# Two transformer blocks on one core: an earlier or later place for three small steps of the experts

## The reference

```python
def peer(xn, w_query, sub_keys, expert_u, expert_v):     # per block of 128 tokens
    q = (xb @ w_query).reshape(128, 8, 2, 128)
    s = einsum('thpc,pkc->thpk', q, sub_keys)
    s1, i1 = top_k(s[:, :, 0], 16); s2, i2 = top_k(s[:, :, 1], 16)
    sc, ci = top_k(s1[..., :, None] + s2[..., None, :], 16)    # of 256 sums
    e = i1[ci // 16] * 128 + i2[ci % 16]                 # one of 16384 experts
    g = softmax(sc)
    act = gelu(einsum('td,thkd->thk', xb, expert_u[e]))
    return einsum('thk,thkd->td', g * act, expert_v[e])
# second block:
    x = x + peer(rms_norm(x, norm2_g), ...)
    return rms_norm(x, final_norm_g)
```

## Time and profile before

| | |
|---|---|
| time, median of 3 runs | 1314.31 us (1312.51 to 1314.51) |
| profiled execution, its own time | 1314.31 us |
| its span, first to last instruction | 1312.5 us |
| mean granted TensorE clock | 0.997 of full speed |
| TensorE busy | 1287.2 us, 98% of the span |
| weight loads of TensorE | 1172.3 us, 89% |
| VectorE / ScalarE / GpSimd busy | 936.6 / 694.5 / 33.8 us |
| transfers | 260.56 MB, mean 199 GB/s |
| last u matmul / first v matmul start | 955.78 / 957.33 us |
| last matmul starts | 1305.43 us |

### The profile page before, as it was taken

The page is one execution under the profiler, slowest core; times in us unless marked ns, Lnnn a source line. Parts: engine busy times, 40 slices in busy tenths (PEclk is TensorE's granted clock), DMA queues, the critical chain, the costliest instruction groups (busy, mean ns, idle before and its releaser), DMA issues.

```text
span 1312.5 us, 22031 instructions
## 1 busy us (share of the span) xinstructions
PE 1287.2 (98%) x8615; PEld 1172.3 (89%) x8615; DVE 936.6 (71%) x1699; ACT 694.5 (53%) x1162; POOL 33.8 (3%) x27
## 2 busy tenths in 40 slices
PE   9999999999999898999999999999999999999997
PEld 8899989998878688999999999999988888888886
DVE  6676567764457655999989777777766666666666
ACT  5565457664455645444454455555554444555554
POOL 0000031000020001000000000000000000000000
PEclk9999999999999999999999999999999999999999
DMA  7443455556656335477777665655677766666663
GB/s 268 156 134 107 140 182 180 188 180 192 192 163 217 112 113 181 145 222 228 231 233 228 204 200 191 201 186 194 203 256 276 242 241 240 240 241 241 242 241 110
DMA packets 72807, 260.56 MB, mean 199 GB/s; under 512 B 8256, under 2 KB 9024, under 8 KB 72448
## 3 DMA queue, kind: packets, MB, share of 16 engines
q1 hardware_dynamic: 71232, 255.25, 59.3%
q0 software_dynamic: 1040, 3.34, 0.8%
q10 hardware_dynamic: 432, 0.56, 0.1%
HBM read 240.25 MB, written 18.87 MB: 197 GB/s over the span
## 4 chain that ended last, share of the span: by engine, by line
PE 91%; ACT 4%; DVE 3%; issue 2%; ACTq 0%; DVEq 0%
PE ps L1072 26%; PE ps L476 14%; PE ps L484 14%; PE ps L485 14%; PE ps L486 14%; PE ps L1055 2%; PE ps L530 1%; ACT whi L1109 1%; PE ps L517 1%; DVE wlo L1590 1%; PE ps L523 1%; ACT TH L1115 1%; PE ps L511 1%; PE ps L999 1%; PE ps L494 0%
## 5 line engine op out<-in xcount | busy, mean ns | idle before, releaser
L1590 DVE TENSOR_TENSOR wlo<-raw,whi 128x1024 fp32r<-128x1024 f32 (+2 forms) x410 | 497.8, 1216 | 309.7 <-ACT whi L1109 307.5
L1109 ACT ACTIVATE whi<-raw 128x1024 fp32r<-128x1024 f32 (+2 forms) x421 | 441.8, 1051 | 414.2 <-PE ps L1072 168.6
L484 PE MATMUL ps<-TH,whi 128*128 128x256 f32 x1504 | 433.0, 288 | 0.0
L485 PE MATMUL ps<-TL,whi 128*128 128x256 f32 x1504 | 426.1, 283 | 0.0
L486 PE MATMUL ps<-TH,wlo 128*128 128x256 f32 x1504 | 426.0, 283 | 0.0
L485 PEld LDWEIGHTS ps<-TL,whi 128*128 128x128 f32 x1504 | 289.1, 192 | 0.0
L484 PEld LDWEIGHTS ps<-TH,whi 128*128 128x128 f32 x1504 | 289.0, 192 | 0.0
L486 PEld LDWEIGHTS ps<-TH,wlo 128*128 128x128 f32 x1504 | 288.8, 192 | 0.0
L1072 PE MATMUL ps<-whi,TH 128*128 128x512 f32 x512 | 199.4, 389 | 1.3 <-issue 1.3
L1072 PE MATMUL ps<-whi,TL 128*128 128x512 f32 x512 | 199.3, 389 | 0.0
L1072 PE MATMUL ps<-wlo,TH 128*128 128x512 f32 x512 | 199.3, 389 | 0.0
(11 more groups left out here) (327 smaller groups left out, 1393.8 us busy)
## 6 DMA issues: line engine op xcount, KB each, us to landing
raw<-in_expert_u_dram SPq DMA_DIRECT2D x128, 512.0 KB, 3.7
raw<-in_expert_v_dram SPq DMA_DIRECT2D x128, 512.0 KB, 3.6
raw<-in_w_up_dram SPq DMA_DIRECT2D x32, 512.0 KB, 3.6
raw<-in_w_down_dram SPq DMA_DIRECT2D x32, 512.0 KB, 4.2
acts<-stage SPq DMA_DIRECT2D x32, 512.0 KB, 4.0
stage<-acts SPq DMA_DIRECT2D x30, 512.0 KB, 3.3
raw<-in_w_in_dram SPq DMA_DIRECT2D x20, 512.0 KB, 4.4
raw<-in_w_gate_dram SPq DMA_DIRECT2D x16, 512.0 KB, 3.5
```

Of the source, the lines that this page charges most:

```text
L484: e.matmul(dst, whi[:, h, sl], xh[:, k, :], start=k == 0, stop=False)
L485: e.matmul(dst, whi[:, h, sl], xl[:, k, :], start=False, stop=False)
L1109: e.activation(whi[:, u % NH, 0:n], raw[:, u % NR, 0:n], ACT.Copy).then_inc(*hi(u))
L1590: e.tensor_tensor(wlo[:, u % NH, 0:n], raw[:, u % NR, 0:n], whi[:, u % NH, 0:n].bitcast(F32), ALU.subtract).then_inc(*lo(u))
```

## The change

It moves instructions; it adds and removes none, apart from semaphore values that follow the new order.

1. TensorE: the products of groups 0 and 1 stood behind the 24 matmuls of unit 66. They now stand behind the first 12 of unit 67; group 2 stays behind unit 67. The loop body became the function `weigh`.
2. VectorE, turn 127: takes 0, 1, 2 and cut 0 now stand ahead of the split of `EV + 1`; cut 1, take 3, cut 2 behind it. On ScalarE the text changes but the order is the same.
3. VectorE, last norm, t = 1: the order was x10, v1, g10, x11, g11 and is now x10, g10, x11, v1, g11. For t = 0 it stays x00, x01, v0, g00, g01.

```diff
         end_d = signal("end_d", (
-            "x00 x01 v0 g00 g01 r0 out01 x10 v1 g10 x11 g11 r1 out11").split())
+            "x00 x01 v0 g00 g01 r0 out01 x10 g10 x11 v1 g11 r1 out11").split())
...
+            def weigh(g):
+                e.wait_ge(*hot.at(g))
+                if g < 4:
+                    if g == 0:
+                        e.wait_ge(*route_a.at("turned0"))
+                    if g == 1:
+                        e.wait_ge(*route_d.at("turned1"))
+                    if g == 2:
+                        e.wait_ge(*route_d.at("turned2"))
+                else:
+                    e.wait_ge(*weight_a.at(g - 4))
+                for i in range(4):
+                    for w in (2, 3):
+                        m = e.matmul(ps[g % 4][:, i * 128:i * 128 + 128], room[:, g % 2, 0, i, :], room[:, g % 2, w, i, :],
+                                     start=w == 2, stop=w == 3)
+                m.then_inc(*weighed(g))
...
                 m = cols(EU + n, 0, 8, TH, TL, ps[b][:, 0:256], range(4))
                 if n == 127:
                     m.then_inc(*half_used("u"))
+                if n == HOT_FROM + 1:
+                    for g in hot_groups(HOT_FROM):
+                        weigh(g)
                 cols(EU + n, 0, 8, TH, TL, ps[b][:, 0:256], range(4, 8)).then_inc(*used(EU + n))
-                for g in hot_groups(n):
-                    e.wait_ge(*hot.at(g))
...
-                    m.then_inc(*weighed(g))
+                if n > HOT_FROM:
+                    for g in hot_groups(n):
+                        weigh(g)
...
                 take_weights(hot_groups(n - 1))
                 if n == 1:
                     score(3)
-                split(EU + n + 2)
                 if n == 127:
+                    split(EV + 1)
                     for i in range(3):
                         cut(i)
+                else:
+                    split(EU + n + 2)
...
                     one_hots(g)
                 if n == 1:
                     score(3)
-                split(EU + n + 2)
                 if n == 127:
-                    take(0)
                     for i in range(3):
-                        take(i + 1)
-                        cut(i)
+                        take(i)
+                    cut(0)
+                    split(EV + 1)
+                    cut(1)
+                    take(3)
+                    cut(2)
+                else:
+                    split(EU + n + 2)
...
             for t in range(2):
                 part, v, s, r = end_st[t]
                 last_sum(t, 0)
-                if t == 0:
-                    last_sum(t, 1)
+                if t == 1:
+                    last_gain(t, 0)
+                last_sum(t, 1)
                 e.wait_ge(*end_a.at(f"{t}0"))
                 mean_eps(v, part[:, 0:1], 1024).then_inc(*end_d(f"v{t}"))
-                last_gain(t, 0)
-                if t == 1:
-                    last_sum(t, 1)
+                if t == 0:
+                    last_gain(t, 0)
                 last_gain(t, 1)
```

## The result

| | before | changed |
|---|---|---|
| time, median (19 runs each) | 1313.03 us | 1310.96 us |
| lowest and highest run | 1312.3, 1318.05 | 1308.94, 1313.18 |
| span of the profiled execution | 1312.5 | 1307.8 |

The ratio is 0.9976, with a 95% interval of 0.9969 to 0.9983: 3.1 us less, give or take 0.9. It is not the ratio of the two medians, which lie 2.07 apart (the means: 1313.85 and 1310.58, 3.28 apart). The runs of each kernel lie in groups, and the median jumps from one to the other: ten of 19 runs before are at 1313.03 or under, nine of 19 changed ones at 1309.75 or under, and the next lies at 1310.96. The spans of the two profiled executions differ by 4.7 us, which is more. The two traces together say where each part of that is.

The account below looks back on a forecast made before the run. TensorE, busy 98% of the span, bounds the kernel, then a short serial chain after its last matmul. 0.91 + 1.43 + 0.05 + 0.73 = 3.1 us off 1314.31 gives 1311.2 us, range 1309.1 to 1312.9.

Parts of the forecast that it names:

- Part 1, 0.91 us: Groups 0 and 1 amid unit 67: 0.91 us gained of 1.21 lost in TensorE's waits; bounds 0.8 to 1.21.
- The short wait for hot(2): TensorE at group 2: a new wait of about 0.3 us, because VectorE's pair for group 2 does not move.
- Interrupting unit 67 costs nothing: TensorE in unit 67: as many switches between one-hot products and u matmuls as before, so priced at nothing.
- Part 2, 1.43 us: Turn from u to v: first weighted values ready before TensorE wants them at 955.90, so the 1.43 us stop goes.
- The chain: Turn 127: takes from 953.81, ScalarE's cut(0) 954.73, VectorE's 955.17 to 955.59, a margin of 0.3 us.
- The first v unit, 0 to 0.14, taken as 0.05: First 12 v matmuls take 2.86 against a mean of 2.72; 0 to 0.14 us may return, 0.05 taken.
- Part 3, 0.73 us: Last norm: with g10 directly after x10, x11 starts at 1305.96, not 1306.69; 0.73 us gained, bounds 0.6 to 0.73.
- v1 behind x11 cost nothing: Last norm: v1 is done by 1306.8, while the root also needs x11's square, which starts at 1306.64 and lasts about 0.6.
- No part failed: Rival, chance 0.15 together: cut(0) still late (1312.6), or the wait moves to VectorE's pairs in units 67 and 68 (1311.7).
- The pair for group 3: VectorE, part 1: hot(3) is ready 0.8 us before its time; 0.5 late would leave part 1 only 0.4.
- The slower case: Rival, chance 0.02: in the v stage the load of EV+5 lands late; a landing of 13.8 us gives 1314.6.
- The chances: Whole kernel: faster 0.65, same 0.32, slower 0.03, with 0.2% (2.6 us) as what can be told from no change.

Follow-up runs that it names:

- best: Changed kernel with both fills, and group 2 moved amid unit 68 as well: median 1307.53 us, ratio to before 0.9952.
- margin: Changed kernel with two more VectorE one-hot comparisons ahead of take(0): last u matmul to first v matmul 0.76 us, against 0.12 changed; no run time given.
- split_second: Changed kernel with turn 127's split of EV+1 after takes 0 to 2 but ahead of cut 0: last u to first v matmul 0.77 us; no run time given.
- fb: Kernel before with filling matmuls of no use in two TensorE gaps (8 near 133, 17 near 448): median 1311.19 us, 8 runs.
- fc: Changed kernel with both sets of filling matmuls, same kernel as fills, run beside fb on one chip: median 1307.93 us, 5 runs.
- p1_only: Kernel before with part 1 of the change alone: median 1313.14 us, ratio to before 0.9997.
- p2_only: Kernel before with part 2 of the change alone (VectorE's turn 127): median 1312.75 us, ratio to before 0.9992.
- p3_only: Kernel before with part 3 of the change alone (the last sum): median 1313.3 us, ratio to before 0.9996.
- groups_late: Changed kernel with groups 0 and 1 behind the whole of unit 67: unit 66's last matmul to group 2 5.13 us, against 4.26 changed; no run time given.
- f133: Changed kernel with only the 8 filling matmuls near 133: median 1309.98 us, 8 runs.
- fp2: Kernel before with part 2 of the change and both sets of filling matmuls: median 1309.71 us, 11 runs.
- fills: Changed kernel with filling matmuls in two TensorE gaps (8 near 133, 17 near 448): median 1307.75 us, ratio to before 0.9953, 5 runs.

## Why the prediction was right, step by step

The forecast was 1311.2 us, 3.1 less. Measured: 1310.96, and by the ratio 3.1 less, or 3.26 without the clock's scatter. The gain was worked out. That the absolute time agrees to 0.2 is luck: the forecast started from 1314.31, the median of three runs, and over 19 runs the median before is 1313.03. From there 3.1 less is 1309.9; the changed kernel's median lies higher because it fell into the upper group of its runs.

- *Part 1, 0.91 us.* Measured 0.91, in the change and alone. The start at 748.59 was forecast for group 0, 1.55 after unit 66's last matmul; it is 1.56. The short wait for hot(2) is there as forecast (0.2 in the view of the waits, 0.36 for the weight loads of the same group); best, where group 2 stands amid unit 68, shows that it is worth 0.3.
- *Interrupting unit 67 costs nothing.* Right: from group 0 to group 2 there is nothing that the sum doesn't have.
- *Part 2, 1.43 us.* Measured 1.43. The chain stood where it was forecast: takes 0.70 after ScalarE's last copy of a group starts (forecast 0.63), ScalarE's cut 1.54 after (1.55), VectorE's cut 1.99 (1.99), its end 0.31 before TensorE wants it (0.31). margin and split_second show by both sides that it is this chain that counts.
- *The first v unit, 0 to 0.14, taken as 0.05.* It is 2.75 in place of 2.83, so 0.08. The 2.86 of the forecast was the length of the window (957.30 to 960.16), not of the unit, which starts at 957.33; so the excess over the mean was 0.11 and not 0.14. The return of all of it, which the prediction drew from the Trainium skill (TensorE: Matmul & The Clock Gate, section "Step-by-step: what each phase is for"), did not happen: even with no stop the first unit is 0.03 slower than the mean. No run here shows why.
- *Part 3, 0.73 us.* The mechanism is right and the size was 0.1 too small: 0.83, outside the bounds of 0.6 to 0.73. I took the release of the last sum as 0.53 after the matmul's start, from the first bank's row. It is 0.43 at most: x11 starts when VectorE is free of g10 (1301.36 + 0.61), no later. With the gain out of the way the release could be earlier still; no run here shows how early. The first bank's sum again starts 0.53 after its last matmul in the changed kernel (1296.77 to 1297.30); why the last bank's comes sooner is open. v1 behind x11 cost nothing, as forecast: it ends at 1302.73 and the root starts at 1303.52.
- *The rivals.* No part failed. The pair for group 3 is ready at 751.73 + 0.69 = 752.42, 0.8 before the group starts (753.23), as forecast. The slower case had no sign: the store that stands behind the load of EV+5 was issued at 954.77, so the load was out by then, and TensorE has no wait in the v stage.
- *The chances.* The gain was expected at 0.5 above the 0.2% that the prediction took for what can be told from no change. It came out near there: 0.24%, with an interval of 0.17 to 0.31%. That is clear of no change, but it reaches below the 0.2%, so these runs alone don't decide between "faster" (0.65) and "same" (0.32) by that bound.
- *What I had not asked.* I took the scatter of 2 us between runs as given. A good part of it had a cause in the trace, and with that out of the way (fb and fc) a change of 3 us in 1310 stood clear of every single run.

## What to carry to other kernels

When an engine is busy without a gap around a stop, the stop is worth its length, and here each part could be forecast to a tenth of a microsecond. What limits it is the chain that comes next: work it out in the same way before naming a price. Moving a dependent step by half a unit can be right where a whole unit is as bad as none, because a chain in the other direction closes.

When the runs of one kernel lie in groups, look at the granted clock window by window before timing more. Comparing distances inside two traces takes such chance out, as long as no fall of the clock lies within them; comparing spans does not. And where runs lie in groups, the difference of two medians can mislead: here it was 2.07, where the ratio gave 3.1, the means 3.28 and the traces 3.26.

## What the runs showed of the hardware

- The granted clock fell behind a gap of 4.29 us of TensorE in every execution profiled without a fill there (before, changed, p1_only, p2_only, p3_only, margin, split_second, groups_late, f133). Behind one of 2.0 us near 133 it fell in four of eight (before, p1_only, p2_only, split_second) and stayed at 1.00 in the other four. Behind one of 1.7 us near 490 it fell in one of fourteen (fp2), at no cost that shows. Unit 66's last matmul starts at 747.08 on average in the four with a fall and at 745.32 in the four without: one fall costs 1.8 us here. The fall near 448 costs 1.1 to 2.1 us by the same mark, against fc, in the executions without a fall near 133. Behind the stops of the expert stages in the kernel before (up to 1.26 us idle) it stayed at 1.00. With the two gaps filled the clock stayed at 1.00 in both places in all five profiles (fills, best, fb, fc, fp2). The Trainium skill, TensorE: Matmul & The Clock Gate, section "What's actually happening", says that the array's default state is the throttled one and that activity releases it; the traces agree as far as they go: the clock fell only behind gaps of TensorE, and with a gap filled it did not fall there. Matmuls whose results nobody reads bought 3.2 us here: 1314.38 (the kernel before, measured beside fb) to 1311.19 (fb), as much as the change itself.
- A wait named by the profile can be that of a neighbour: "issue" in margin and the split in split_second both stood for VectorE's subtraction, which had ended 0.10 us before.
- VectorE starts its next operation before the last one's recorded end: the three takes of the changed kernel are 0.34 apart and last 0.42 each, and the split (953.15) starts 0.34 after the first subtraction (952.81), which lasts 0.42.
